# A decoder step in two layers: the first layer's last column pair in three runs of tokens, and the state space stage takes the squares of the last 128

## The reference

```
h = h + rms_norm(mixer(rms_norm(h, g0)), g1)
h = h + rms_norm(sq_relu_mlp(rms_norm(h, g2), w1, w2), g3)

def sq_relu_mlp(x, w1, w2):          # w1: 1024 x 4096, w2: 4096 x 1024
    h = relu(x @ w1)
    return (h * h) @ w2

def s5_mix(xn, h0, ...):             # xn is the normalized stream of layer 1
    bu = einsum(b_bar, u)            # u: xn in 64 groups of 16 channels
    h  = scan over tokens            # complex, 64 states in each group
    y  = gelu(real(einsum(c, h)) + d * u)
    return y * sigmoid(y @ w_glu + b_glu), last state
```

## Time and profile before

| | |
|---|---|
| median of three runs | 1537.56 us (1537.48 to 1539.92) |
| the profiled execution | 1539.29 us |
| its span, first to last instruction | 1537.6 us |
| TensorE busy | 1479.6 us, 96% of the span |
| VectorE, ScalarE, GpSimd busy | 872.6, 422.5, 354.4 us |
| mean granted TensorE clock | 0.985 |
| last column pair, half 1, last product ends | 978.5 us from the start |
| first transpose of `hT` in the state space stage | 984.4 us |

### The profile page before, as it was taken

One profiled execution on the slowest core, in us unless ns is written; L12 is line 12 of the kernel. 1 busy time (PEld: TensorE's weight loads), 2 busy tenths in 40 slices (PEclk: granted clock), 3 DMA queues, 4 the chain that ended last, 5 costly groups with the idle time before them and its releaser, 6 DMA issues. The chain is left out here.

```text
span 1537.6 us, 25820 instructions
## 1 busy us (share of the span) xinstructions
PE 1479.6 (96%) x9697; PEld 1226.2 (80%) x9697; DVE 872.6 (57%) x1926; ACT 422.5 (27%) x1076; POOL 354.4 (23%) x478
## 2 busy tenths in 40 slices
PE   8999899888898999999999999899999999999998
PEld 7878799555464788888888888678888888888888
DVE  2654343677653777555567743780385556676513
ACT  3011243677630172333300000434341111000012
POOL 0000300455552219995000008271000000000000
PEclk9999899899998999999999999999999999999999
DMA  8445461301197623644343420523122313222201
GB/s 271 129 109 140 154 209 52 107 26 56 42 303 262 183 82 126 222 152 141 141 137 123 133 98 9 233 98 118 55 70 95 110 55 110 93 97 85 83 28 56
DMA packets 142893, 184.34 MB, mean 120 GB/s; under 512 B 31298, under 2 KB 101642, under 8 KB 141746
## 3 DMA queue, kind: packets, MB, share of 16 engines
q1 hardware_dynamic: 139634, 174.31, 34.4%
q0 software_dynamic: 3136, 8.39, 1.6%
HBM read 163.42 MB, written 29.69 MB: 126 GB/s over the span
## 5 line engine op out<-in xcount | busy, mean ns | idle before, releaser
L2567 POOL TENSOR_SCALAR att_p<-att_p,att_tot,gates 128x512 f32<-128x512 f32 (+3 forms) x128 | 79.8, 636 | 67.6 <-DVE att_tot L2489 67.6
L294 PE MATMUL psum<-xT,l_w 128*128 128x260 f32 x384 | 87.2, 388 | 4.8 <-ACT nsa_y L493 2.8
L294 PEld LDWEIGHTS psum<-xT,l_w 128*128 128x128 f32 x384 | 73.9, 193 | 17.2 <-ACT nsa_y L493 3.2
L951 PE MATMUL psum<-xT,l_w 128*128 128x260 f32 x384 | 85.2, 383 | 1.6 <-PEq L113 1.6
L951 PEld LDWEIGHTS psum<-xT,l_w 128*128 128x128 f32 x384 | 72.8, 190 | 12.9 <-issue 1.8
L967 PE MATMUL psum<-l_up_t,l_w_sums 128*128 128x260 f32 x336 | 78.2, 382 | 0.0
L2482 DVE CUSTOM_DVE_ANT_0 att_p<-psum,causal 128x512 f32<-128x512 f32 (+3 forms) x128 | 57.5, 486 | 35.9 <-PE psum L2328 35.4
L2140 PE MATMUL psum<-cmp_xt,cmp_w 64*128 64x256 f32 (+2 forms) x640 | 74.8, 371 | 0.4 <-DVE cmp_xt L2064 0.4
L2537 ACT ACTIVATE att_p<-att_p,att_low 128x512 f32<-128x512 f32 (+3 forms) x128 | 70.8, 557 | 4.6 <-DVE att_low L2482 4.1
L967 PEld LDWEIGHTS psum<-l_up_t,l_w_sums 128*128 128x128 f32 x336 | 63.8, 190 | 9.8
L2328 PE MATMUL psum<-att_kT,qrT 64*128 64x512 f32 (+3 forms) x256 | 55.2, 510 | 14.1 <-DVE att_low L2482 13.9
(11 more groups left out here) (584 smaller groups left out, 3195.7 us busy)
## 6 DMA issues: line engine op xcount, KB each, us to landing
l_w<-in_mlp_w SPq DMA_DIRECT2D x16, 2048.0 KB, 8.0
l_w<-in_mlp_w SPq DMA_DIRECT2D x32, 1024.0 KB, 5.1
proj_w<-in_nsa_w_in SPq DMA_DIRECT2D x4, 2048.0 KB, 10.1
cmp_raw<-in_cache_kv_cmp SPq DMA_DIRECT2D x24, 256.0 KB, 3.0
xT<-in_cache_kv_cmp SPq DMA_DIRECT2D x24, 256.0 KB, 2.9
sa_more<-in_cache_kv_sel POOLq DMA_DIRECT2D x44, 128.0 KB, 6.5
sa_more<-in_cache_kv_sel SPq DMA_DIRECT2D x34, 128.0 KB, 7.5
hT<-in_cache_kv_cmp SPq DMA_DIRECT2D x16, 256.0 KB, 2.9
```

The costliest lines, as they stand in the source:

```text
L294: mm = nc.tensor.matmul(ps[:, n % 8, 0:HALF], w[s][:, k, m * P:(m + 1) * P], src[:, kk, cols(h)], start=(kk == 0), stop=(kk == last))
L951: mm = nc.tensor.matmul(ps[:, n % 8, 0:HALF], w[s][:, k, m * P:(m + 1) * P], src[:, kk, cols(h)], start=(kk == 0), stop=(kk == last))
L2567: ve.tensor_scalar(pr[:, n % PR, par, 0:w], pr[:, n % PR, par, 0:w], tot[:, n % PR, par:par + 1], c.gates[:, i, gate:gate + 1], ALU.mult, ...
```

## The change

The last column pair's tokens go in three runs: `RUNS[0]` is tokens 260 to 519 (260 wide), `RUNS[1]` 128 to 259 (132), `RUNS[2]` 0 to 127 (128). So the old half order is turned round: the upper half comes first, then the lower half in two pieces. Each run has two banks, the sums of squares of the first two share bank 7.

On TensorE run 0 is as half 0 was. Run 1 goes column tile by column tile, with run 0's sum behind its first chunk. Run 2 goes chunk by chunk with both column tiles, and run 1's sum stands behind its first chunk. Run 2's sum comes last. On VectorE each run is keep, add, keep, add, then `join_run`, all of it before the next run's first keep; `dve_clear` stands ahead of the join of run 1. The squares of the new `hT` are taken in this stage for runs 0 and 1; the state space stage takes those of the last 128 columns worked on, tokens 0 to 127, and adds them to `hacc[:, 0, 0:P]`. Its waits count two runs of joins, 16 tiles, in place of 8, and `turn_states` waits for the second root. SyncE's load of `tz` waits for six filled banks, and the pieces of `ssm_vt` for the chunks of run 2.

```
-    LAST_BANKS = {(0, 0): 0, (0, 1): 1, (1, 0): 2, (1, 1): 6}
-    SUM_BANKS = {"mix": (0, 4), "down": (7, 4)}
+    RUNS = [slice(HALF, T), slice(P, HALF), slice(0, P)]
+    LAST_BANKS = [(0, 1), (3, 5), (2, 6)]
+    SUM_BANKS = {"mix": (0, 4), "down": (7, 7, 4)}
...
-            sp.wait_ge(last_filled, 4)
+            sp.wait_ge(last_filled, 6)
...   TensorE
+            def last_products(run, m, chunk):
+                wt, lo, hi = down_slot(STEPS + chunk)
+                at = (lo, hi)[m]
+                for k in range(CK):
+                    kk = chunk * CK + k
+                    mm = nc.tensor.matmul(ps[:, LAST_BANKS[run][m], 0:width(run)], wt[:, k, at:at + P], hid[:, kk, RUNS[run]],
+                                          start=(kk == 0), stop=(kk == KF - 1))
+                if chunk == NCHUNK - 1:
                     mm.then_inc(last_filled, 1)
-                return mm
+                elif run == 2 and m == 1:
+                    mm.then_inc(h_taken, 1)
+
+            def sum_run(run):
+
+                pe.wait_ge(added["down"], 2 * (LAST + run) + 2)
+                nc.tensor.matmul(ps[:, SUM_BANKS["down"][run], 0:width(run)], c.ones[:], of_run(acc, run), start=True, stop=True).then_inc(summed["down"], 1)
...
             pe.wait_ge(down_joined, 7 * PASSES)
             for m in range(2):
                 for chunk in range(NCHUNK):
-                    for k in range(CK):
-                        mm = last_product(1, m, chunk, k)
-                    if m == 1 and chunk < NCHUNK - 1:
-                        mm.then_inc(h_taken, 1)
+                    last_products(1, m, chunk)
                     if m == 0 and chunk == 0:
-                        sum_squares("down", 0, 2 * MF - 2)
-            sum_squares("down", 1, 2 * MF)
+                        sum_run(0)
+            for chunk in range(NCHUNK):
+                for m in range(2):
+                    last_products(2, m, chunk)
+                if chunk == 0:
+                    pe.wait_ge(rooted["down"], 1)
+                    sum_run(1)
+            sum_run(2)
             ssm.pe(pe)
...   ScalarE
-            square_y(2 * LAST)
-            square_y(2 * LAST + 1)
-            root("down", 0)
-            feed("down", 0, 0, 8)
-            square_y(2 * LAST + 2)
-            square_y(2 * LAST + 3)
-            root("down", 1)
+            for run in range(3):
+                for m in range(2):
+                    square_last(run, m)
+                root_run(run)
+                if run < 2:
+                    square_run(run)
             ssm.act(act)
...   VectorE
+            def keep_last(run, m):
+
+                dve.wait_ge(last_filled, 2 * run + m + 1)
+                ve.tensor_mul(y[:, LAST + m, RUNS[run]], ps[:, LAST_BANKS[run][m], 0:width(run)], of_run(hrs, run)).then_inc(y_scaled, 1)
+
+            def add_last(run, m):
+
+                n = 2 * (LAST + run) + m
+                dve.wait_ge(squared["down"], n + 1)
+                dve.wait_ge(added["down"], n)
+                ve.tensor_add(of_run(acc, run), of_run(acc, run), sq[:, n % 2, 0:width(run)]).then_inc(added["down"], 1)
+
+            def join_run(run):
+
+                factor, sums, where = of_run(rs, run), of_run(hacc, run), RUNS[run]
+                dve.wait_ge(rooted["down"], run + 1)
+                ve.reciprocal(factor, factor).then_inc(recip["down"], 1)
+                dve.wait_ge(recip["down"], run + 1)
+                dve.wait_ge(y_scaled, 2 * (LAST + run) + 2)
+                for s in range(KD + (3 if run < 2 else 1)):
+                    if s < KD:
+                        ve.scalar_tensor_tensor(y[:, s, where], y[:, s, where], gain(3, s), factor, ALU.mult, ALU.mult).then_inc(scaled["down"], 1)
+                    if 1 <= s <= KD:
+                        dve.wait_ge(scaled["down"], run * KD + s)
+                        ve.tensor_add(c.hT[:, s - 1, where], c.hT[:, s - 1, where], y[:, s - 1, where]).then_inc(joined["down"], 1)
+                    if s >= 3 and run < 2:
+                        ...   # adds the square of tile s - 3 to sums
...
-            keep_last(0, 0)
-            keep_last(0, 1)
-            for n in (2 * LAST, 2 * LAST + 1):
-                add_down(n)
-            inverse("down", 0)
-            dve.wait_ge(y_scaled, 2 * LAST + 2)
-            join("down", 0, 0, KD + 3)
-            keep_last(1, 0)
-            add_down(2 * LAST + 2)
-            ssm.dve_clear(dve)
-            keep_last(1, 1)
-            add_down(2 * LAST + 3)
-            inverse("down", 1)
-            dve.wait_ge(y_scaled, 2 * LAST + 4)
-            join("down", 1, 0, KD + 1)
+            for run in range(3):
+                for m in range(2):
+                    keep_last(run, m)
+                    add_last(run, m)
+                if run == 1:
+                    ssm.dve_clear(dve)
+                join_run(run)
             ssm.dve(dve)
...   state space stage
-        self.squares = at("ss_squares", [P, 6, HALF], 103744)
+        self.squares = at("ss_squares", [P, 6, P], 103744)
-            pe.wait_ge(self.rooted, 1)
+            pe.wait_ge(self.rooted, 2)
-            pe.wait_ge(self.joined, KD + k + 1)
+            pe.wait_ge(self.joined, 2 * KD + k + 1)
-            nc.scalar.activation(self.squares[:, k % 6], c.hT[:, k, HALF:], ACT.Square).then_inc(self.h_squared, 1)
+            nc.scalar.activation(self.squares[:, k % 6], c.hT[:, k, 0:P], ACT.Square).then_inc(self.h_squared, 1)
-        nc.vector.tensor_add(c.hacc[:, 1], c.hacc[:, 1], late).then_inc(self.h_ready, 1)
+        nc.vector.tensor_add(c.hacc[:, 0, 0:P], c.hacc[:, 0, 0:P], late).then_inc(self.h_ready, 1)
```

More of the change, by code:

```diff
@@ L231, in y_tile, with of_run, width @@
         r, i = divmod(n, 4)
-        return 2 * r + ((0, 1, 1, 0) if r < PASSES else (0, 1, 0, 1))[i], i // 2
+        return 2 * r + (0, 1, 1, 0)[i], i // 2
+    def of_run(buf, run):
+        return buf[:].rearrange("p h t -> p (h t)")[:, RUNS[run]]
+    def width(run):
+        return RUNS[run].stop - RUNS[run].start
     with nc.Block() as block:
@@ L462, in _ @@
                 pe.wait_ge(d_landed[d % 4], 16 * (d // 4 + 1))
-                for m in range(2):
-                    if chunk == 0 and m == 1:
-                        pe.wait_ge(down_joined, 7 * (PASSES - 1) + 1)
-                    for k in range(CK):
-                        last_product(0, m, chunk, k)
+                last_products(0, 0, chunk)
+                if chunk == 0:
+                    pe.wait_ge(down_joined, 7 * (PASSES - 1) + 1)
+                last_products(0, 1, chunk)
             pe.wait_ge(down_joined, 7 * PASSES)
@@ L499, in square_y, with square_last, root_run, square_run @@
                 square("down", n, y[:, tile, cols(h)])
+            def square_last(run, m):
+                n = 2 * (LAST + run) + m
+                act.wait_ge(y_scaled, n + 1)
+                act.wait_ge(added["down"], n - 1)
+                nc.scalar.activation(sq[:, n % 2, 0:width(run)], y[:, LAST + m, RUNS[run]], ACT.Square).then_inc(squared["down"], 1)
+            def root_run(run):
+                act.wait_ge(summed["down"], run + 1)
+                nc.scalar.activation(of_run(rs, run), ps[:, SUM_BANKS["down"][run], 0:width(run)], ACT.Sqrt, bias=c.eps[:]).then_inc(rooted["down"], 1)
+            def square_run(run):
+                for k in range(KD):
+                    act.wait_ge(joined["down"], run * KD + k + 1)
+                    if run * KD + k >= 2:
+                        act.wait_ge(h_added["down"], run * KD + k - 1)
+                    nc.scalar.activation(hsq[:, k % 2, 0:width(run)], c.hT[:, k, RUNS[run]], ACT.Square).then_inc(h_squared["down"], 1)
             def root(r, h):
@@ L630, in join @@
                         ve.tensor_add(c.hT[:, k, cols(h)], c.hT[:, k, cols(h)], y[:, k, cols(h)]).then_inc(joined[r], 1)
-                    if s >= 3 and (r, h) != ("down", 1):
+                    if s >= 3:
                         k = s - 3
@@ new lines, in add_last @@
+            def add_last(run, m):
+                n = 2 * (LAST + run) + m
+                dve.wait_ge(squared["down"], n + 1)
[14 more added lines that the diff above has]
+                    if s >= 3 and run < 2:
+                        k = s - 3
+                        dve.wait_ge(h_squared["down"], run * KD + k + 1)
+                        if k:
+                            dve.wait_ge(h_added["down"], run * KD + k)
+                            ve.tensor_add(sums, sums, hsq[:, k % 2, 0:width(run)]).then_inc(h_added["down"], 1)
+                        else:
+                            ve.tensor_copy(sums, hsq[:, k % 2, 0:width(run)]).then_inc(h_added["down"], 1)
@@ L3853, in dve @@
         for n, k in enumerate((6, 7)):
[L3854 removed]
+            dve.wait_ge(self.h_squared, 2 * KD + k + 1)
             if n:
```

22 lines of the change are left out of this document (6 added, 16 removed).

## The result

The changed kernel took 1542.85 us (median of 14 runs), the kernel before 1536.62 on the same chips. The ratio is 1.0039, with a 95% interval from 1.0028 to 1.0050: slower by 6.0 us (4.3 to 7.7). The forecast was slower by 4.5, 1542.1. That the absolute times lie 0.75 us apart is partly luck: the forecast stood on a median of 1537.56 for the kernel before, and the longer series has 1536.62. The difference, 6.0 against 4.5, is the fair comparison.

The account below looks back on a forecast made before the run. TensorE, busy 96% of the span, was taken as the bound. Later last product +5.9, shorter tail -1.9, clock losses +1.4, clock regained -0.9 gave +4.5 us: 1542.1 against 1537.56, range 1538.6 to 1544.3.

Parts of the forecast that it names:

- Run 0 unchanged: First run of the last column pair: same instructions as the old first half, nothing changes until TensorE finishes it at 949.83.
- TensorE's own work: Products of the last two runs, narrower than the old second half: 28.65 us in place of 28.06, +0.6.
- First wait: TensorE at the first run's sum waits 1.3 us for VectorE's adds, held by GpSimd; bounds 0 and 1.7.
- Second wait: TensorE at run 1's sum waits 3.4 us for squares made after the preceding GpSimd-held join; bounds 2.9 and 4.0.
- Tail: From last product to state space stage: steps at 128 tokens, not 260, save 1.9 us (1.6 to 2.1), leaving 4.0.
- Clock in run 2: Half clock on the last run's products after the 3.4 us wait: up to 3.4 us of products, loss taken as 1.4.
- Clock in the tail: At the first transposes, the shorter tail may keep the clock up: 0 to 2.5 us back, 0.9 taken.
- a sign that it was wrong: Granted clock of 1.0 at the first transposes, named beforehand as one observation that would show the prediction wrong.
- rival A: Tail's clock decides: full clock at the first transposes (2.5 back), no clock loss earlier; +1.5, 1539.1, not slower; 10%.
- Sum: Whole kernel: later last product, shorter tail and both clock terms add to +4.5 us, 1542.1 against 1537.56.
- After the first transposes nothing is shorter: State space stage: narrower squares, GpSimd adds and joins are already hidden, counted as nothing (bounds 0 and -0.4).
- Rival E: State space stage: the old one hid a bound taken for TensorE's order, so the change is faster by 2 to 4; 3%.

Follow-up runs that it names:

- run 1: Not a follow-up kernel: the changed kernel's second token run in the last column pair, tokens 128 to 259 (132 wide); no time of its own.
- the filled wait: Changed kernel with 14 extra unread identity products (28 instructions) in front of run 1's sum: 1539.56 us, ratio 1.0019.
- the changed kernel with the short table: Changed kernel with the last of six rounds of GpSimd's rotation table replaced by a fill with zeros: 1534.72 us, ratio 0.9987.
- The busy tail: Changed kernel reordered (run 1's squares inside the preceding join, dve_clear earlier), plus 4 and 5 unread identity products in the tail's gaps: 1533.92 us, ratio 0.9977.
- the kernel before with a busy tail: Kernel before with 5 and 10 extra unread identity products in the two gaps of its tail: 1540.29 us, ratio 1.0023.

## Why the prediction was right, step by step

The step that the forecast rests on, that a join held by GpSimd comes out from behind the shorter block of products and TensorE waits for it, was right in mechanism and size. Two terms of the clock were not. The forecast of +4.5 stood 1.5 us too low, and its own narrower range (+3 to +6) ended where the measurement lies; only the wide one held it clearly.

- *Run 0 unchanged.* Right: 30.02 us for its 128 instructions and the 16 of run 1 behind them.
- *TensorE's own work, +0.6.* Right: run 1 and the first chunk of run 2 are 144 instructions in 16.33 us, (16.33 - 0.28)/143 = 0.1122 apart; at full clock 96 of run 2 take 10.88 (the filled wait), (10.88 - 0.28)/95 = 0.1116. By the Trainium skill, page "TensorE: Matmul & The Clock Gate", section "Back-to-back issue gap", the loss would have been an estimated 6.4 us, some ten times that; the measurement decides against it for these pairs of float32 instructions.
- *First wait, 1.3.* Measured 1.21 by the profile. The add took 2.00 us beside GpSimd's operation, as read. What I didn't say is that this wait is worth nothing by itself: the sum of run 1 stands at a time that GpSimd sets, and moving the sum of run 0 changed it by 0.02 us.
- *Second wait, 3.4.* Measured 3.42. Its cause is shown: with GpSimd's last round out of the way it is gone, and so is the loss. That an earlier or later start of the join doesn't move its end is shown only over a small span: the join started 32.71, 32.47 and 32.80 us after the start of the pair (before, changed, run 0's sum later) and run 1's or half 1's first keep came at 49.45, 49.53 and 49.55.
- *Tail, 1.9 us shorter.* Measured 5.88 - 3.92 = 1.96.
- *Clock in run 2, +1.4, bounds 0 and 1.7.* This term was mis-sized: 2.4 us. I took the length of the half clock from the one stretch of the earlier trace rows, 3.4 us. The old tail, whose rows I quoted in the same group, had 6.8, and so had run 2: from 969.95 to 976.7, of which 5.6 us held the sum and products. The upper bound should have come from the longer row.
- *Clock in the tail, -0.9.* Measured -0.66 (10.48 to 9.82 from the first transpose to the sum of squares). The number is near by luck. The prediction let the shorter tail either lower the clock as before or spare it, and took a middle; it called a clock of 1.0 at the first transposes a sign that it was wrong. That sign came: the clock there was 1.00. But it fell at 990.4 all the same, with TensorE busy since 988.90, so the fall was only put off, and of the 2.5 us of rival A 0.66 came. Another execution with the same tail can have none of it: the changed kernel with the short table had waits of 1.05 and 1.28 there, as this one, and took 10.79. The busy tail shows that 2.1 are to be had (8.39).
- *Sum.* 5.9 - 1.9 + 1.4 - 0.9 = +4.5 was forecast; by the trace it is 4.6 of waits (1.21 + 3.42), 0.6 of narrower products, 0.7 for the sums (0.54 and 0.58 from each to the next product, where the old one took 0.44), 0.4 at the places where a wait now breaks the stream of products, 2.4 of clock, -1.96 of tail, -0.66 of clock in the tail = +6.05. The timed difference is 6.0. Of the 1.5 missing from the forecast 1.0 is the clock in run 2, 0.4 the sums and the stream's ends, 0.2 the clock in the tail. In the trace with run 0's sum alone one chunk later, run 2 lost 1.44 by the clock and the term would have been right. Which of the two lengths of the earlier trace rows would come, 3.4 or 6.8, those rows don't say.
- *After the first transposes nothing is shorter.* Right for these two kernels, and only because TensorE was slow there: the kernel before with a busy tail shows that VectorE's join lies close beneath it (a wait of 2.29). Rival E pointed at this bound; it doesn't show in the change itself.

## What to carry to other kernels

A step that hides behind another engine's products is hidden by the length of those that stand ahead of the place where its result is waited for. Before halving a block, put the time at which the hidden step ends (with every hold on it, here GpSimd's) against the time at which the shorter block ends; the sum of the parts of a tail says nothing of that. A wait of TensorE inside a stream of products can cost more than its length (3.42 us cost 2.4 more in half clock; the waits of 1.21 and 1.14 cost nothing more), and products that nobody reads, in exactly the wait, can give the rest back, but only where no other engine lies close beneath. And a wait taken out of one place moves to the next engine without slack: three orders were needed until VectorE had its join, its memset and its keeps in the right places.

## What the runs showed of the hardware that I had not expected

- After a wait of 3.42 us the granted clock was half for 6.8 us, 5 of them uninterrupted products; with one of 4.92 us it was half for 3.4, and the 96 products took 12.32 us, a loss of 1.4. The loss behind a wait is not a function of its length alone.
- With 28 matmul instructions on the identity in the wait, which left 0.21 us of it, the clock stayed full. With 18 in the gaps of the tail, where waits of 0.29 and 0.25 us were left, it stayed full too; with 20 there and 1.14 us left it fell.
- A VectorE operation on two SBUF tiles that meets a GpSimd operation on 1024 elements ends just behind it: 0.43 us became 2.00, and a chain of them went at one operation to each GpSimd instruction. VectorE's product of a PSUM bank with an SBUF tile, started in the middle of such a GpSimd instruction on 512 elements (944.42 against 944.30 to 945.35), took its usual 0.43. That it is the PSUM operand that spares it isn't shown, since no such product met a GpSimd operation on 1024 elements. VectorE's reciprocal, which reads one SBUF tile, did (952.07 against 950.56 to 952.54 and 952.61 to 954.97) and took the same 1.78 as without GpSimd; and an add of two SBUF tiles beside GpSimd's fill of 1024 elements, in the kernel with the short table, took 0.43.

Open: the timed differences and the distances agree within the intervals but not beyond; for the kernel before with a busy tail they are 3.5 (0.8 to 6.1) and 1.5 us. What decides how long the half clock lasts (3.4 or 6.8 us here) the runs don't show. From the sum of squares to the second layer's first product the kernels with three runs need 0.35 us more (66.8 against 66.4); it stands 63 us behind the sum, where TensorE waits 1.24 us for VectorE in place of 0.88. I didn't follow that up.
